# The sample's attention over quarters of the keys, with keys turned in 32x32 blocks by VectorE

## The chip, the cores and the metric

One core of a Trainium2 chip runs the whole program. The metric is the time of one execution in device microseconds; three runs of the kernel before took 3929.97, 3932.57 and 3942.89, their median is 3932.57 us.

## The reference

One step of a hybrid decoder layer: a prompt of 2048 rows and a sample group of 8 sequences with 4 new tokens each, both through the same weights. Only the sample's sparse attention matters here. For each of the 8 sequences it scores the 4 new tokens against 4096 cached keys, which lie in 32 pages of 128, and the 4 new ones; an indexer leaves 256 keys of 4100 to each token, the others get a score of minus infinity.

```python
s = jnp.einsum('bqkgd,bqnkd->bqkgn', qg, ks) * (A_HEAD_DIM ** -0.5)
s = jnp.where(valid[:, :, None, None, :], s, -jnp.inf)
p = jax.nn.softmax(s, axis=-1)
o = jnp.einsum('bqkgn,bqnkd->bqkgd', p, vs)
...
y_a = y_a * jax.nn.silu(zg_a)
```

There are 8 heads over 2 key heads of 64 features. A page holds, for each of its 128 keys, 128 floats of keys and 128 of values (both key heads), 1 KB a key, 128 KB a page. The kernel keeps all keys and adds to each score a bias that is 0 where the indexer selected the key and a very negative number elsewhere.

## The kernel before

The program is a row of stages, each closed by a barrier of all engines (`Stage.__exit__`, L100): the front (projections and indexer), the bias stage `stage_sample_bias` (L2331), the prompt's attention, the sample's attention `stage_sample_attend` (L2361), the prompt's RWKV, the sample's RWKV, and the merge. The change rewrites the second and the fourth of these; all else stays.

The bias stage has the indexer's selection as `part`, 128 partitions: 4 quarters of 1025 keys by 32 rows (8 sequences by 4 tokens). It copies the quarters side by side (L2352), turns them on TensorE in 33 pieces (L2345) and copies the result to `bias_t` with a key per partition (L2357).

The sample's attention goes sequence by sequence, in loops of the sequencers over two rounds of 4 buffers. A sequence's 32 pages come in through two queues, SyncE and GpSimd, 16 pages each: four page numbers are read from the table in SBUF into registers (L2398), then four DMAs follow (L2401). TensorE turns the 32 key blocks of 128x128 (L2444) in groups of four, ScalarE copies each group to SBUF as `kt` (L2485). For the scores (L2453) the turned keys of a page are the weights and the 32 query rows (4 tokens by 8 heads; zeros keep the key heads apart) are the 32 columns that stream, so a score has the key on the partition. VectorE adds the bias (L2524), takes the maximum over the pages (L2531); TensorE turns the maxima (L2458) and spreads the result over the partitions (L2460); VectorE subtracts (L2537), ScalarE takes the exp (L2489), VectorE sums (L2540). For the values (L2464) the probabilities of a page are the weights, 32 columns wide, and the page's values stream, 128 columns. A sequence's output is divided by its sum and the half of its own key head is kept (L2542 to L2546). After the last sequence GpSimd writes the output to DRAM and reads it back in another layout (L2427, L2429), TensorE turns it (L2472), and VectorE multiplies by the gate and writes `y_s` (L2553).

TensorE's order is written out for four sequences: the keys of sequence i + 1 are turned behind the scores of i, and the values of i follow behind that. Each engine works its list in order and waits on semaphores.

Of the kernel before, what the change touches and what calls it, by code (L numbers as in the profile page):

```python
# [16 lines left out]
NS = SB * ST  # L17
# [2313 lines left out]
def stage_sample_bias(nc, t, k, part, bias_t):  # L2331

    NPG = PAST // PAGE
    with Stage(nc, "sbi") as s:
        sc = s.sb("sc", [NS, L_S])
        turn = s.ps("turn", [P, 2048])
        step, joined, turned = s.sem("step"), s.sem("joined"), s.sem("turned")
        block = s.block()

        @block.tensor  # L2340
        def _(pe):
            pe.wait_ge(joined, 1)
            for c in range(NPG + 1):
                n = P if c < NPG else ST
                last = pe.transpose(turn[0:n, c * NS:(c + 1) * NS], sc[:, c * P:c * P + n], k.ident[0:NS, 0:NS])  # L2345
            last.then_inc(turned, 1)

        @block.vector
        def _(dve):
            chain = Chain(dve, step)  # L2350
            for at, keys in QUARTERS:
                chain.mark(dve.tensor_copy(sc[:, keys], part[at, :]))  # L2352
            chain.mark(dve.memset(bias_t[:, NPG, :], LOW))
            chain.catch_up()
            dve.sem_inc(joined, 1)
            dve.wait_ge(turned, 1)
            chain.mark(dve.tensor_copy(bias_t[:, 0:NPG, :], turn[:, 0:NPG * NS].rearrange("p (n c) -> p n c", c=NS)))  # L2357
            chain.link(dve.tensor_copy(bias_t[0:ST, NPG, :], turn[0:ST, NPG * NS:(NPG + 1) * NS]))


def stage_sample_attend(nc, t, k, z_s, bias_t, y_s):  # L2361

# [3 lines left out]
    NK = NPG + 1  # L2366
    BUFS = 4
    with Stage(nc, "sat") as s:
        oc = nc.dram_tensor("sat_oc", [SB, NS, HD], F32).ap()
        table = s.sb("table", [1, SB * NPG], I32)  # L2370
        kv = [s.sb(f"kv{i}", [P, NPG, 2 * P]) for i in range(BUFS)]
        kt = [s.sb(f"kt{i}", [P, NPG, P]) for i in range(2)]
        q_all, qb = s.sb("q_all", [P, SB, ST, KVH, G]), s.sb("qb", [P, NS])
        k_new, v_new = s.sb("k_new", [P, ST]), s.sb("v_new", [ST, SB, P])
        sm, pt = s.sb("sm", [P, NK, NS]), s.sb("pt", [P, NK, NS])
        mx, mrow, diag, top = s.sb("mx", [P, NS]), s.sb("mrow", [NS, 1]), s.sb("diag", [NS, NS]), s.sb("top", [P, NS])
        ones, v_b = s.sb("ones", [P, P]), s.sb("v_b", [ST, P])
        part, inv = s.sb("part", [P, NS]), s.sb("inv", [NS, 1])
        own, o_m, o = s.sb("own", [NS, P]), s.sb("o_m", [NS, P]), s.sb("o", [NS, SB, HD])
        row = s.sb("row", [NS, 1], I32)  # L2380
        rowf = s.sb("rowf", [NS, 1])
        ya, zg, th, gate = s.sb("ya", [NS, RW]), s.sb("zg", [P, 4, NS]), s.sb("th", [P, 4, NS]), s.sb("gate", [P, 4, NS])
        ptr = s.ps("ptr", [P, 1024])
        ps = s.ps("ps", [P, 1536])
        pm, po, pd = s.ps("pm"), s.ps("po"), s.ps("pd")
        tab_in, kv_in, kv_free, vn_in, made = s.sem("tab_in"), s.sems("kv_in", BUFS), s.sems("kv_free", BUFS), s.sem("vn_in"), s.sem("made")
        kv_in2 = s.sems("kv_in2", BUFS)
        sem = {n: s.sem(n) for n in ("set_up", "step", "qb_ok", "turned", "copied", "scored", "masked", "mxd", "mx_t", "dg",
                                     "topp", "cent", "expd", "summed", "pvd", "dend", "o_ok", "stored", "ya_in", "yt", "thd",
                                     "pages", "pages2")}  # L2390
        S = sem
# [3 lines left out]
        def load_pages(eng, done, it, i, half):  # L2395

            with eng.Fori(0, NPG // 8) as n:
                pages = [eng.value_load(table[0:1, bass.ds(it * (BUFS * NPG) + n * 4 + (i * NPG + half * (NPG // 2) + a), 1)],  # L2398
                                        min_val=0, max_val=NPH - 1) for a in range(4)]
                for a, page in enumerate(pages):  # L2400
                    eng.dma_start(kv[i][:, bass.ds(n * 4 + (half * (NPG // 2) + a), 1), :],  # L2401
                                  kv_rows[bass.ds(page, 1), :, :].rearrange("o p c -> p o c")).then_inc(done, 16)

        @block.sync
        def _(sp):
# [3 lines left out]
            for i in range(BUFS):  # L2409
                sp.sem_inc(kv_free[i], 1)  # L2410
            with sp.Fori(0, SB // BUFS) as it:
                for i in range(BUFS):
                    sp.wait_ge(kv_free[i], it + 1)
                    sp.sem_inc(S["pages"], 1)
                    load_pages(sp, kv_in[i], it, i, 0)
# [16 lines left out]
        def _(pe):  # L2432
            pe.wait_ge(S["set_up"], 1)
            pe.wait_ge(vn_in, 16)
            with pe.Fori(0, SB // BUFS) as it:
# [11 lines left out]
                for i in range(BUFS):  # L2447
# [7 lines left out]
                    if i + 1 < BUFS:  # L2455
                        turn(i + 1)
# [444 lines left out]
```

## Time and profile before

| | us |
|---|---|
| median of three runs | 3932.57 |
| the profiled execution | 3935.04 |
| its span in the profile | 3933.5 |
| PE busy | 3477.9 (88%) |
| DVE busy | 2146.5 (55%) |
| ACT busy | 1127.3 (29%) |
| POOL busy | 568.7 (14%) |

The span runs from the first to the last instruction of the profiled execution, and the 1.5 us beside it are the start and end of the execution. PE counts TensorE's matmuls, PEld its weight loads, which can run beside them. A float32 matmul leaves two records each of PE and PEld, one for each of its passes, a transpose one. PEclk is the clock that was granted to TensorE, as a share of 2.4 GHz. A row of a timeline merges neighbours of one form: "x64" are 64 records, and the time is that from the first start to the last end; the end of a matmul is modelled and holds the way through the array, which the next one overlaps.

### The profile page before, as it was taken

The page shows a single profiled execution, that of the slowest core. Times are in us where ns is not written, and L with a number is a line of the kernel's source. Part 1 is how long each engine was busy: PE and PEld are TensorE (multiplying, and loading weights), DVE is VectorE, ACT ScalarE, POOL GpSimd, SP SyncE. Part 2 cuts the span into 40 slices and gives each one's busy share as a digit, 9 for nine tenths or more (in the row PEclk, how much of TensorE's full clock was granted, in tenths as well). Part 3 has the DMA queues.
Part 4 walks back from the last instruction along what each step waited for, and adds up shares of the span by engine and source line. Part 5 has one row for each costly group of instructions (what it writes and reads, how often), then busy time and mean ns, then how long its engine had stood idle before and what let it go on. Part 6 is the DMA issues. An engine that isn't in the chain of part 4 may idle for free. (4 is left out here: it accounts for less than half of the span.)

```text
span 3933.5 us, 73267 instructions
## 1 busy us (share of the span) xinstructions
PE 3477.9 (88%) x29021; PEld 2124.0 (54%) x29021; DVE 2146.5 (55%) x4190; ACT 1127.3 (29%) x2375; POOL 568.7 (14%) x728
## 2 busy tenths in 40 slices
PE   8999999999999989999957858889871199999998
PEld 4444455555555545555547746667661165555653
DVE  2038899999999957666612235555543622222221
ACT  4236620000000004444411225555531021111221
POOL 3320000000000000000023013343432410000000
PEclk9999999999999998999966767666765599999999
DMA  4231111111111112110045111111114121111110
GB/s 147 69 104 46 39 56 53 60 55 58 55 59 54 60 55 54 25 25 17 7 132 171 43 31 38 43 39 39 37 22 175 36 77 62 56 58 60 48 48 22
DMA packets 209587, 229.62 MB, mean 58 GB/s; under 512 B 27178, under 2 KB 185317, under 8 KB 208773
## 3 DMA queue, kind: packets, MB, share of 16 engines
q1 hardware_dynamic: 150744, 119.10, 10.7%
q0 software_dynamic: 22672, 57.08, 5.2%
q10 hardware_dynamic: 35868, 49.13, 3.5%
q8 instruction: 224, 3.67, 0.4%
q14 instruction: 79, 0.64, 0.1%
HBM read 156.65 MB, written 68.59 MB: 57 GB/s over the span
## 5 line engine op out<-in xcount | busy, mean ns | idle before, releaser
L409 PE MATMUL fro_acc<-h_t,fro_w 128*128 128x416 f32 x3280 | 1174.2, 516 | 0.0
L409 PEld LDWEIGHTS fro_acc<-h_t,fro_w 128*128 128x128 f32 x3280 | 614.8, 190 | 542.6 <-issue 535.6
L692 DVE TENSOR_SCALAR_CACHE_REDUCE fro_work<-scores,fro_real 128x384 uint8<-128x384 f32 (+6 forms) x462 | 656.2, 1474 | 2.1
L516 ACT ACTIVATE fro_out<-fro_acc 128x416 f32<-128x416 f32 (+3 forms) x230 | 118.0, 513 | 794.6 <-PE fro_acc L409 711.8
L2786 DVE CUSTOM_DVE_ANT_0 att_seen<-att_ps,scores 128x512 f32<-128x512 f32 (+3 forms) x320 | 182.6, 608 | 119.9 <-PE att_ps L2675 119.3
L2021 PE MATMUL mrg_po<-wo,mrg_mrg 128*128 128x512 f32 (+1 forms) x544 | 236.5, 593 | 1.4 <-DVE mrg_mrg L2115 1.4
L2049 PE MATMUL mrg_pg<-wg,mrg_x_t 128*128 128x512 f32 (+1 forms) x544 | 236.3, 592 | 0.0
L658 DVE SCALAR_TENSOR_TENSOR scores<-fro_work,w_idx,scores 128x512 f32<-128x512 f32 (+3 forms) x280 | 187.9, 671 | 39.2 <-ACT fro_work L573 12.2
L2711 PE MATMUL att_po<-att_prob_t,att_v 128*64 128x128 f32 x2176 | 184.6, 288 | 2.1 <-ACT att_prob_t L2773 1.0
L2688 PE MATMUL att_pt<-ident,att_seen 128*128 128x128 f32 x1088 | 184.2, 291 | 1.5 <-ACT att_seen L2756 1.5
L2711 PEld LDWEIGHTS att_po<-att_prob_t,att_v 128*64 128x64 f32 x2176 | 113.9, 137 | 115.7 <-issue 83.0
L2675 PE MATMUL att_ps<-att_kt,att_qt 64*128 64x512 f32 (+3 forms) x640 | 164.5, 593 | 13.4 <-DMA att_qt<-z_t 13.4
L2021 PEld LDWEIGHTS mrg_po<-wo,mrg_mrg 128*128 128x128 f32 (+1 forms) x544 | 100.6, 185 | 134.4 <-issue 132.6
L573 ACT ACTIVATE fro_work<-fro_wk 128x512 f32<-128x512 f32 (+3 forms) x320 | 144.5, 540 | 90.9 <-PE fro_wk L482 90.0
L2049 PEld LDWEIGHTS mrg_pg<-wg,mrg_x_t 128*128 128x128 f32 (+1 forms) x544 | 100.6, 185 | 125.6 <-issue 124.8
L2756 ACT ACTIVATE att_seen<-att_seen,att_shift 128x128 f32<-128x128 f32 (+15 forms) x128 | 152.5, 1193 | 31.0 <-DVE att_shift L2794 29.9
L2121 DVE SCALAR_TENSOR_TENSOR mrg_th<-mrg_th,mrg_pw 128x1024 f32<-128x1024 f32 (+1 forms) x17 | 20.7, 1220 | 239.7 <-ACT mrg_th L2093 239.7
L2773 ACT ACTIVATE att_prob_t<-att_pt 128x512 f32<-128x512 f32 (+1 forms) x148 | 81.8, 553 | 242.2 <-PE att_pt L2688 242.2
L1990 POOL DMA_DIRECT2D mrg_m_in<-z_t x72 | 51.1, 710 | 678.7 <-DVE mrg_mrg L2115 676.0
L2688 PEld LDWEIGHTS att_pt<-ident,att_seen 128*128 128x128 f32 x1088 | 115.7, 142 | 56.5 <-issue 45.6
L2651 POOL MEMSET att_sel<- 8x512 f32 x1 | 0.5, 514 | 1004.5 <-POOLq L100 1004.5
L2005 PE MATMUL mrg_br<-mrg_y_in,wr 128*128 128x256 f32 (+2 forms) x576 | 126.4, 363 | 13.4 <-DMA mrg_y_in<-y_t 13.4
(428 smaller groups left out, 4947.4 us busy)
## 6 DMA issues: line engine op xcount, KB each, us to landing
z_t<-fro_out ACTq DMA_DIRECT2D x180, 208.0 KB
fro_w<-in_w_in SPq DMA_DIRECT2D x41, 512.0 KB, 4.2
sat_kv<-in_cache_kv SPq DMA_DIRECT2D x128, 128.0 KB, 2.3
sat_kv<-in_cache_kv POOLq DMA_DIRECT2D x128, 128.0 KB, 2.7
mrg_m_in<-z_t POOLq DMA_DIRECT2D x56, 256.0 KB, 3.2
z_t<-fro_out ACTq DMA_DIRECT2D x45, 192.0 KB
scores<-in_x_prompt SPq DMA_DIRECT2D x16, 512.0 KB, 8.3
mrg_x<-in_x_prompt SPq DMA_DIRECT2D x16, 512.0 KB, 3.4
```

The costliest lines, as they stand in the source:

```text
L409: last = pe.matmul(acc[e % 2][:, 0:CW], w[block_no % 3][:, kk, :], h_t[:, kk, CW * g:CW * g + CW], start=(kk == 0), stop=(kk == KD - 1))
L573: act.activation(rel[m % 8][:, 0:width], wk[m % 6][:, 0:width], ACT.Relu).then_inc(relued, 1)
L658: ins = dve.scalar_tensor_tensor(o, rel[m % 8][:, 0:width], wh, o, ALU.mult, ALU.add)
L692: chain.mark(dve.tensor_scalar(junk[b % 2][:, 0:n], scores[:, c:c + n], realf[:, b:b + 1], None, op, ALU.add, accum_out=count[:, b:b + 1]))
L2005: last = pe.matmul(br[:, d % 2, W * a:W * a + m], w[:, c, d * P:(d + 1) * P], y_in[g % 2][:, a, c, 0:m], start=(c == 0), stop=(c == 3))
L2021: last = pe.matmul(po[0:n, 512 * h:512 * h + 512], mrg[g % 2][:, c, o:o + n], wo[:, c, 512 * h:512 * h + 512], start=(c == 0), stop=(c == ...
L2049: last = pe.matmul(pg[0:n, 512 * h:512 * h + 512], x_t[:, c, 0:n], wg[:, c, 512 * h:512 * h + 512], start=(c == 0), stop=(c == KD - 1))
L2675: last = pe.matmul(ps[z % 2][e][:, 0:width], qt[b % 2][w, hh, :], kt[w, 512 * sl:512 * sl + width], start=True, stop=True)
L2688: last = pe.transpose(pt[i % 2][:, 256 * e + P * a:256 * e + P * a + P], seen[n % 3][e][:, P * kb:P * kb + P], k.ident[:, :])
L2711: last = pe.matmul(po[b % 2][64 * e:64 * e + 64, P * hh:P * hh + P], v[:, kb, 64 * e:64 * e + 64], prob_t[i % 4][:, 256 * e + P * a:256 * ...
L2756: act.activation(row, row, ACT.Exp, bias=shift[n % 3][:, e:e + 1], scale=scale, accum_out=total[b % 2][:, 4 * e + hh:4 * e + hh + 1]).then ...
L2786: dve.tensor_tensor_reduce(seen[n % 3][e][:, 512 * sl:512 * sl + width], ps[z % 2][e][:, 0:width], scores[:, c:c + width], 1.0, -3.4e38, A ...
```

## The change

The bias keeps its rows as partitions. A quarter of the 4096 keys belongs to each group of 32 partitions (rows (sequence, token)), so the bias stage only shifts the quarters of 1025 to quarters of 1024 and clamps them at -1e30; TensorE has no part in it.

The scores now have (quarter, token, head) on the 128 partitions and a quarter's 1024 keys on the free axis, in 4 banks of 256; a 257th column of each bank takes one of the 4 new keys. For a sequence, TensorE

- writes the bias to the score tile: 16 matmuls on the four diagonal 32x32 tiles, with a 0/1 matrix `sel` as weights that repeats a token's bias for its 8 heads;
- adds the scores: 64 matmuls with 32 query features as rows, 32 query rows as columns, and 256 keys streaming. The turned keys come from VectorE, which turns each 32x32 block where it stands, so that features lie on every group of 32 partitions; partition group n holds the keys 32n to 32n + 31 of every page, in every block f of 32 features;
- adds the new keys' scores (4 matmuls of one column).

VectorE takes one maximum per partition, over its own quarter alone; ScalarE takes one exp over all of it, which sums at once (`accum_out`). Nine transposes bring the probabilities to keys on partitions, ScalarE copies them, and the values are 32 matmuls on four column tiles, a quarter each. A sequence's four partial outputs are kept in `parts`. After the last sequence the quarters are weighed by the exp of their maximum against the row's, added by a matmul with four unit blocks (`same`), divided, and turned to `y_s` in SBUF, without the way through DRAM.

Three queues load the pages: of each quarter's 8 pages SyncE takes 3, GpSimd 3, ScalarE 2. There are 3 buffers of a whole sequence instead of 4, and one `kt` instead of two. The loops over sequences are written out. Numbers of lines in the order below are those of the changed file.

```diff
-            for at, keys in QUARTERS:
-                chain.mark(dve.tensor_copy(sc[:, keys], part[at, :]))
...
+            for g in range(4):
+                chain.mark(dve.tensor_scalar(whole[at[g], g:QK], part[at[g], 0:QK - g], FAR, None, ALU.max))
...
+            chain.mark(dve.tensor_copy(bias[:, :, 0:256].rearrange("p k (x i) -> p k x i", i=32),
+                                       whole[:, 0:QK].rearrange("p (x k i) -> p k x i", k=4, i=32)))
...
-    BUFS = 4
+    BUFS = 3
+    GP = NPG // 4
+    SHARE = (slice(0, 3), slice(3, 6), slice(6, 8))
...
+        def load_pages(eng, b, who):
+            i, mine = b % BUFS, SHARE[who]
+            if b >= BUFS:
+                eng.wait_ge(weighed, b - BUFS + 1)
+                eng.wait_ge(turned, 4 * (b - BUFS) + 4)
+            for g in range(4):
+                at = [GP * g + a for a in range(mine.start, mine.stop)]
+                pages = [eng.value_load(table[0:1, NPG * b + a:NPG * b + a + 1], min_val=0, max_val=NPH - 1) for a in at]
...
         @block.tensor
...
+                pe.transpose(po[0:ST, 256:256 + P], prob_n[b % 2][:, :], k.ident[:, :]).then_inc(flip_n, 1)
+                for x in range(GP):
+                    last = pe.transpose(tp[:, P * x:P * x + P], prob[b % 2][:, x, :, :].rearrange("p k i -> p (k i)"), k.ident[:, :])
...
+                pe.wait_ge(copied, 3 * b + 3)
+                for x in range(GP):
+                    for g in range(4):
+                        pe.matmul(po[rows(g), 0:P], pt[:, x, rows(g)], kv[i][:, GP * g + x, P:2 * P], start=(x == 0),
+                                  stop=(x == GP - 1 and g < 3), skip_group_check=True)
...
+            for b in range(SB):
+                if b:
+                    pe.wait_ge(exped, b)
+                    pe.wait_ge(exp_n, b)
+                for n in range(4):
+                    for g in range(4):
+                        last = pe.matmul(ps[rows(g), n, 0:257], sel[rows(g), ST * b:ST * b + ST, :].rearrange("p t h -> p (t h)"),
+                                         bias[rows(g), n, :], start=True, stop=False, skip_group_check=True)
...
+                if b:
+                    weigh(b - 1)
...
+                for g in range(4):
+                    pe.wait_ge(turned, 4 * b + g + 1)
+                    for f in range(4):
+                        for n in range(4):
+                            pe.matmul(ps[rows(g), n, 0:256], qd[rows(n), b, f, :], kt[rows(n), GP * g:GP * g + GP, 32 * f:32 * f + 32],
+                                      start=False, stop=(f == 3), skip_group_check=True)
...
         @block.scalar
...
+            for b in range(SB):
+                act.wait_ge(peaked, b + 1)
+                act.activation(prob[b % 2][:, :, :, :].rearrange("p x k i -> p k x i"), ps[:, :, 0:256].rearrange("p k (x i) -> p k x i", i=32),
+                               ACT.Exp, bias=less[:, b:b + 1], scale=float(HD ** -0.5), accum_out=sum_a[:, b:b + 1]).then_inc(exped, 1)
...
+                if b + 2 < SB:
+                    load_pages(act, b + 2, 2)
...
         @block.vector
...
+                    if b and g == 0:
+                        dve.wait_ge(scored, b)
+                    dve.transpose(kt[:, GP * g:GP * g + GP, :], kv[b % BUFS][:, GP * g:GP * g + GP, 0:P]).then_inc(turned, 1)
+                if b:
+                    keep(b - 1)
+                dve.wait_ge(scored, b + 1)
+                chain.link(dve.tensor_reduce(most[:, b:b + 1], ps[:, :, 0:257], AX.XY, ALU.max))
+                dve.tensor_scalar(less[:, b:b + 1], most[:, b:b + 1], -float(HD ** -0.5), None, ALU.mult).then_inc(peaked, 1)
```

TensorE's list before, from the last keys of a sequence to the scores of the next (`sat_ptr` holds turned keys, `sat_ps` scores, `sat_pm` maxima, `sat_po` outputs; ISA and REGISTER_ALU rows set registers of the loop):

```order
L2444 MATMUL sat_ptr<-ident,sat_kv 128x128 x4
L2458 MATMUL sat_pm<-ident,sat_mx 32x128
L2460 MATMUL sat_pm<-sat_diag,sat_ones 128x32
L2461 REGISTER_ALU
L2462 ISA
L2464 MATMUL sat_po<-sat_kv,sat_pt 32x128 x32
L2465 MATMUL sat_po<-sat_v_b,sat_pt 32x128
L2469 MATMUL sat_pd<-sat_ones,sat_part 32x1
L2449 REGISTER_ALU
L2451 ISA
L2453 MATMUL sat_ps<-sat_qb,sat_kt 128x32 x32
L2454 MATMUL sat_ps<-sat_qb,sat_k_new 4x32
```

The same list now, the first sequence's scores, then the second's bias, the first's values, and the second's scores (`sat_tp` holds turned probabilities):

```order
L2453 MATMUL sat_ps<-bias_t,sat_sel 32x257 x16
L2463 MATMUL sat_ps<-sat_kt,sat_qd 32x256 x64
L2466 MATMUL sat_ps<-z_s,sat_qf 32x1 x4
L2453 MATMUL sat_ps<-bias_t,sat_sel 32x257 x16
L2432 MATMUL sat_po<-ident,sat_prob_n 4x128
L2434 MATMUL sat_tp<-ident,sat_prob 128x128 x8
L2440 MATMUL sat_po<-sat_kv,sat_pt 32x128 x32
L2442 MATMUL sat_po<-sat_v_new,sat_pt_n 32x128
L2463 MATMUL sat_ps<-sat_kt,sat_qd 32x256 x64
```

The key turning has left TensorE, the 32 wide score matmuls became 16 + 64 small ones, and the values of a sequence stand between the bias and the scores of the next.

ScalarE's list now, from a sequence's exp to the first of the eight page loads for the sequence after the next (before, it held eight copies of turned keys and an exp, and no DMA):

```order
L2494 ACTIVATE sat_prob,sat_sum_a<-sat_ps,sat_less 128x4x8x32
L2496 ACTIVATE sat_prob_n,sat_sum_b<-sat_ps,sat_less 128x4
L2501 ACTIVATE sat_pt_n<-sat_po 4x128
L2504 ACTIVATE sat_pt<-sat_tp 128x512 x2
L2403 TENSOR_LOAD sat_table
L2403 ISA x2
L2403 TENSOR_LOAD sat_table
L2403 ISA x2
L2405 ISA
L2405 DMA sat_kv<-in_cache_kv 128x256
```

The loads moved to a queue that also holds the exp of the next sequence, behind them.

## Rows read from the trace of the kernel before

**Rows 1.** Windows: us, busy (count) of PE, PEld, DVE, ACT, POOL, PEclk, DMA share, GB/s.
```profile
1993.70:2314.60 320.90, 228.98 (x1356) 205.15 (x1356) 71.11 (x131) 45.85 (x73) 70.08 (x131) 0.69 0.35 105
1998.80:2021.50 22.70, 0.00 (x0) 0.00 (x0) 0.49 (x3) 0.00 (x0) 8.66 (x17) 0.50 0.61 186
...
2208.70:2221.00 12.30, 12.25 (x66) 12.13 (x66) 0.00 (x0) 0.00 (x0) 0.00 (x0) 0.58 0.00 0
2231.20:2240.00 8.80, 8.78 (x65) 8.04 (x66) 1.85 (x1) 0.00 (x0) 0.00 (x0) 0.81 0.00 0
2362.00:2364.00 2.00, 1.92 (x64) 1.69 (x64) 0.11 (x2) 1.99 (x5) 0.00 (x0) 0.50 0.15 42
```

**Rows 2.** Timeline of one sample: start us, us, engine line op out<-in.
```profile
2208.75 12.17 PE L2453 MATMUL sat_ps<-sat_qb,sat_kt 128*128 128x32 f32 x64 [2.22 <-DVEq L2520]
...
2221.06 6.25 PE L2444 MATMUL sat_ptr<-ident,sat_kv 128*128 128x128 f32 x32
2221.36 1.23 DVE L2524 TENSOR_TENSOR sat_sm<-sat_ps,bias_t 128x1024 f32<-128x1024 f32 x1 [12.90 <-PE sat_ps L2454]
...
2222.70 1.97 DVE L2531 TENSOR_REDUCE sat_mx<-sat_sm 128x32 f32<-128x1056 f32 x1
...
2230.01 1.08 ACT L2489 ACTIVATE sat_pt<-sat_sm 128x1056 f32<-128x1056 f32 x1 [2.07 <-DVE sat_sm L2537]
...
2231.22 8.76 PE L2464 MATMUL sat_po<-sat_kv,sat_pt 128*32 128x128 f32 x64 [2.77 <-ACT sat_pt L2489]
...
2242.88 12.17 PE L2453 MATMUL sat_ps<-sat_qb,sat_kt 128*128 128x32 f32 x64 [2.22 <-DVEq L2520]
```

**Rows 3.** Timeline of the page loads on SyncE and GpSimd.
```profile
1998.76 111.36 SPq L2401 DMA_DIRECT2D sat_kv<-in_cache_kv  x82
...
2004.43 2.48 POOL L2401 DMA_DIRECT2D sat_kv<-in_cache_kv  x4 [3.10 <-issue]
2009.98 2.48 POOL L2401 DMA_DIRECT2D sat_kv<-in_cache_kv  x4 [3.06 <-issue]
```

**Rows 4.** Timeline of the stage's end.
```profile
2307.88 0.15 DVE L2542 RECIPROCAL sat_inv<-sat_pd 32x1 f32<-32x1 f32 x1 [8.69 <-PE sat_pd L2469]
...
2314.25 0.29 DVE L2553 SCALAR_TENSOR_TENSOR y_s<-sat_pd,sat_gate 128x128 f32<-128x128 f32 x1 [4.88 <-PE sat_pd L2472]
```

**Rows 5.** Costliest groups on VectorE: shapes, count, busy us, mean ns, idle.
```profile
L1744 DVE STREAM_TRANSPOSE rwk_pw<-rwk_ta 128x256 f32<-128x256 f32 x64 | 28.0, 437 | 58.5 <-ACT rwk_ta L1542 58.5
```

**Rows 6.** Chain that ended last, in the merge: start us, us.
```profile
3200.96 13.73 PE mrg_pg L2049 x32
```

**Rows 7.** Timeline of TensorE, four stretches with small tiles.
```profile
188.34 1.14 PE L445 MATMUL fro_wk<-fro_work,fro_qs 32*32 32x512 f32 x32
...
227.20 3.74 PE L461 MATMUL fro_wk<-scores,fro_sel 128*32 128x512 f32 x48
...
299.81 1.14 PE L482 MATMUL fro_wk<-fro_work,fro_qi 32*128 32x512 f32 x8
300.88 2.36 PE L409 MATMUL fro_acc<-h_t,fro_w 128*128 128x416 f32 x6
...
2362.08 1.93 PE L1312 MATMUL rwk_zz<-rwk_ta,rwk_pw 32*32 32x64 f32 x64 [1.86 <-DVE rwk_pw L1744]
```

**Rows 8.** Timeline of ScalarE in the prompt's attention.
```profile
1950.42 0.60 ACT L2773 ACTIVATE att_prob_t<-att_pt 128x512 f32<-128x512 f32 x1 [1.64 <-PE att_pt L2688]
...
1951.00 2.00 ACT L2756 ACTIVATE att_seen<-att_seen,att_shift 128x2048 f32<-128x2048 f32 x1
...
1952.91 0.19 ACT L2756 ACTIVATION_READ_ACCUMULATOR att_seen<-att_seen,att_shift 128x1 f32 x1
```

**Rows 9.** Timeline of the bias stage.
```profile
1456.74 2.83 DVE L2352 COPY sbi_sc<-part 32x1025 f32<-32x1025 f32 x4 [27.67 <-PEq L100]
...
1463.43 1.22 DVE L2357 COPY bias_t<-sbi_turn 128x1024 f32<-128x1024 f32 x1 [3.82 <-PE sbi_turn L2345]
```

**Rows 10.** Tile sat_po: min/median/max ns, first and last start.
```profile
L2464 PEld LDWEIGHTS sat_po<-sat_kv,sat_pt x512: 109/110/178, 2055.0 to 2306.8; 128*32 128x32 f32 x171
```

More of the change, by code:

```diff
@@ L2328, in _, with stage_sample_bias @@
             g.finish(dve, 0, y_s[0][:, :, :])
-def stage_sample_bias(nc, t, k, part, bias_t):
-    NPG = PAST // PAGE
+FAR = -1.0e30
+def stage_sample_bias(nc, t, k, part, bias):
+    QK = PAST // 4
     with Stage(nc, "sbi") as s:
-        sc = s.sb("sc", [NS, L_S])
-        turn = s.ps("turn", [P, 2048])
-        step, joined, turned = s.sem("step"), s.sem("joined"), s.sem("turned")
+        whole = s.sb("whole", [P, QK + ST])
+        step = s.sem("step")
         block = s.block()
[L2340 to L2346, printed above, removed]
         @block.vector
@@ L2386, in stage_sample_attend @@
[L2386 to L2391, printed above, removed]
+        kt = s.sb("kt", [P, NPG, P])
@@ new lines, in stage_sample_attend @@
+        qd, qf, sel = s.sb("qd", [P, SB, 4, NS]), s.sb("qf", [P, SB, ST, KVH, G]), s.sb("sel", [P, SB * ST, AH])
+        v_new = s.sb("v_new", [ST, SB, P])
+        prob, prob_n = [s.sb(f"prob{i}", [P, GP, 4, 32]) for i in range(2)], [s.sb(f"prob_n{i}", [P, ST]) for i in range(2)]
+        pt, pt_n = s.sb("pt", [P, GP, P]), s.sb("pt_n", [ST, P])
+        most, less, sum_a, sum_b = s.sb("most", [P, SB]), s.sb("less", [P, SB]), s.sb("sum_a", [P, SB]), s.sb("sum_b", [P, SB])
+        parts, same = s.sb("parts", [P, SB, P]), s.sb("same", [P, NS])
@@ L2392, in stage_sample_attend, with rows @@
         block = s.block()
         kv_rows = t["cache_kv"][0].rearrange("n p a h d -> n p (a h d)")
[L2395 to L2402, printed above, removed]
+        def rows(g):
+            return slice(32 * g, 32 * g + 32)
@@ L2408, in _ @@
             sp.wait_ge(tab_in, 16)
[L2409 to L2415, printed above, removed]
+            for b in range(SB):
+                load_pages(sp, b, 0)
         @block.gpsimd
@@ new lines, in _ @@
+            weigh(SB - 1)
+            pe.wait_ge(peaked, SB)
+            pe.transpose(end[0:SB, 0:P], most[:, :], k.ident[:, :]).then_inc(m_turned, 1)
+            pe.wait_ge(peak_ok, 2)
+            pe.matmul(end[:, 256:256 + SB], peaks[:, :, :].rearrange("b g q -> b (g q)"), k.ident[0:SB, 0:SB], start=True, stop=True)\
+              .then_inc(spread, 1)
+            pe.wait_ge(all_w, 3)
+            for h in range(2):
+                pe.matmul(tp[0:NS, 512 * h:512 * h + 512], same[:, :], parts[:, 4 * h:4 * h + 4, :].rearrange("p b c -> p (b c)"),
+                          start=True, stop=True)
@@ L2507, in _ @@
+            chain.catch_up()
+            for n in range(1, 4):
+                chain.mark(dve.tensor_copy(qd[rows(n), :, :, :], qd[0:32, :, :, :]))
             dve.wait_ge(made, 1)
```

261 lines of the change are left out of this document (120 added, 141 removed).

## The prediction

> **What bounds the kernel now.** I read the table of windows first, to see how much of the span the edited stage holds and which engine fills it. The sample's attention runs from 1993.7 to 2314.6 us, 321 us of 3933.5; TensorE is busy for 229 of them, at a mean granted clock of 0.69, between its two levels of 1.2 and 2.4 GHz, and the DMA engines for 0.35 [rows 1]. A stage is closed by a barrier of all engines, so what the stage loses the kernel loses: nothing of another stage runs beside it.
>
> The timeline of one sample comes next, after the DMAs are over [rows 2]. Seen from one row L2453 to the next, 2208.75 to 2242.88, a sample takes 34.1 us, and its parts stand one after another: scores 12.17, turning the next sample's keys 6.25, then maximum, subtraction and exp on VectorE and ScalarE, values 8.76. The scores are 32 matmuls of only 32 columns (64 records: every float32 matmul leaves two, its two passes). They bring a full 128x128 weight each, and PEld is busy for 12.13 of 12.30 us [rows 1]. So they are paid in weight loads.
>
> The third view is the page loads [rows 3]. GpSimd issues four pages in 5.55 us (2004.43 to 2009.98), 1.39 a page, SyncE 82 in 111.4, 1.36 a page. A sample of 32 pages over two queues thus takes 16 x 1.39 = 22 us. The first waits for it (1998.8 to 2021.5, TensorE idle, DMA share 0.61 [rows 1]), the others don't, since 34 is more than 22.
>
> **The change part by part.** Removed per sample are TensorE's key turning with its eight copies, the 64 records of scores, the 64 of values, VectorE's sum pass and column maxima, the transposes of the maxima. Per stage goes the round trip of the output through DRAM, part of the 6 us from L2542 to y_s [rows 4]. Added is the following, per sample.
>
> *Turned keys.* Four VectorE transposes of 128x1024. The trace has the same operation at 128x256, 437 ns [rows 5]; its first 1024-column neighbour is L2524, 1.23 us for 1024 elements. I take 437 + 768 x (1230 / 1024) ns = 1.36, ends 1.23 and 4 x 0.437 = 1.75, so 5.4 us. They begin when the scores before them are read and the maximum is taken (the key buffer is single), 1.4 us into the cycle, and end at 6.8. TensorE asks for them at 11 or later, so they cost nothing; at 1.75 apiece they end at 8.4 and still do not.
>
> *TensorE.* The price of a pass is that of L2049: 32 records of 512 columns in 13.73 us, 0.429 each, 0.84 ns a column at full clock [rows 6]. The question is how many tiles share a pass. Four 32-row matmuls of 512 columns (eight records of L482) take 1.14 us; one after another they would take 8 x 0.429 = 3.4. Sixteen 32x32 matmuls (32 records of L445) also take 1.14. Four 32-column tiles under all 128 rows (L461, 48 records) take 3.74 for eight rounds of 512 columns, which is 0.43 a round plus 0.3 for sixteen one-column records [rows 7]. So tiles that differ in rows or columns run together, and I count rounds:
> - bias, 16 matmuls of 257 columns on the four diagonal tiles: 4 rounds x 2 passes x 257 x 0.84 ns = 1.7 us;
> - scores, 64 of 256 columns. Within a group of output rows the four row tiles run together, but the four feature blocks follow each other on the same tile: 16 rounds x 2 x 256 x 0.84 = 6.9. Were all 16 tiles fed at once it would be 1.7, were none shared 27.5; L445 and L482 were issued so that no tile came twice, hence the middle;
> - nine transposes of 128 columns in one pass, 1.0; values, 8 rounds x 2 x 128 x 0.84 = 1.7, and 0.1 for the new tokens; the four one-column matmuls 0.3;
> - changes of tile shape. From L482 (299.81) to the next L409 (300.88) are 1.07, where two passes are 0.86, so 0.2 out and back; some 0.15 each, five of them, 0.7.
>
> That is 12.4 us at full clock, 24.8 at half. At the stage's present mean of 0.69 it is 18.0. I take that: the new matmuls stream more columns per weight load, which speaks for more, and the waits below speak for less. Before, the values, which stream 128 columns, ran at 0.81 and the scores at 0.58 [rows 1].
>
> *Where TensorE waits.* The score tile is single too, so from the last score to the next bias stand VectorE's maximum over 1028 PSUM columns (1.23, as L2524; at the 1.97 of L2531 at the dearest), the scaling 0.17, an exp of 1024 (half of L2756's 2.00 us), its accumulator read 0.19, the small exp with its own read 0.4, and four hand-overs of 0.1 (L2489 ends at 2231.09, L2464 begins at 2231.22): 3.4 us [rows 2, 8]. After the transposes it waits for ScalarE's last copy, 0.60 (L2773), and hand-overs, 1.0. So 4.4, and a cycle is 18.0 + 4.4 = 22.4 us.
>
> *Queues.* SyncE and GpSimd now issue 12 pages a sample and ScalarE 8. At the old price that is 12 x 1.39 = 16.7 us, under 22.4; the share of DMA time would rise from 0.61 at 22 us a sample to 0.8. ScalarE's 8 pages, 11.1 us, stand in its queue behind the copies and ahead of the next exp. That is covered by the values (2.6 at this clock), the scores (10) and the maximum (1.4), 14 us; without that cover the next exp is late by the difference.
>
> *Bias stage.* It has four copies from 1456.74 (2.83 us), 33 transposes on TensorE, and from 1463.43 the copies back, which end at 1464.7 [rows 9], so 8 us. The new one stays on VectorE: four passes like the four copies, seven tiny ones (0.1 each), one copy of 1024 (1.22): 5 us, 3 less.
>
> *Sum.* The first sample's pages are in after 16.7 + 2 us, at 2018; its last quarter of turning (1.4) and of scores (3.5 at the half clock that the idle engine has there, 0.50 [rows 1]) ends at about 2023. Seven cycles of 22.4 are 157. Then 3.4 for exp, 1.0 for the copy, (1.0 + 1.8 + 0.4) / 0.69 = 4.7 for the last values. The join is a chain of some 16 short steps: two VectorE passes of 1024 (1.25 each), three of 512 (0.6), four 512-column records (0.86 to 1.7), eight transposes and nine steps of 0.2 to 0.4 with hand-overs, 11 us, 4 more than the old end. y_s is written at 2023 + 157 + 9 + 11 = 2200 instead of 2314.5, 114 less; with the bias stage 117. The profiled execution took 3935.0, so 3818; the median of the runs shown is 2.5 lower, so **3816**. Two prices that no row shows: clearing more semaphores at the stage's end (0 to 1 us), and fetching code that is now written out rather than looped (0, by L445, which is written out too and puts 32 loads and 32 matmuls into 1.14 us; at the most the 0.3 that L461 has over its rounds, per sample [rows 7]).
>
> **A rule against the change.** Consecutive score rounds load new weights into the same tiles. L1312 does just this, eight times two passes on four tiles with 64 columns: 64 records in 1.93 us [rows 7] at a granted clock of 0.50 [rows 1], where 16 passes x 64 columns x 1.67 ns are 1.71. What is left, 0.22, is paid once, not per pass, so the loads are hidden and my sum has none. The Trainium skill, TensorE: Matmul & The Clock Gate, Part 3 on packing, says that a weight load overlaps matmuls in flight only where its row group is another; by that the 32 score passes would each show theirs. The trace disagrees, in that row.
>
> **The rivals.**
> 1. *The clock stays at half.* For it: 4.4 us of waits in each cycle, and L1312 at 0.50. Then 24.8 + 4.4 = 29.2, seven are 204, and 2024 + 204 + 24 = 2252: 65 less, **3867**. Against it: the values' 0.81.
> 2. *The clock is full, and the queues bound.* 12.4 + 4.4 = 16.8 against 16.7 of issuing; 2023 + 118 + 18 = 2159, 159 less, **3774**. For it: the merge's L2049 streams at full clock; against it, the waits.
> 3. *Weight loads stand between the passes.* A load of 32 columns takes 0.11 us, 0.18 at the longest (L2464 on PEld [rows 10]); 32 of them are 3.5 to 5.7 a sample, 25 to 40 over seven, **3848**. Against it: L1312. It is what the skill's rule above would give.
> 4. *Slower: tiles on the same output rows do not share a pass.* The four row tiles of a score round add into the same partitions, in four banks, round after round, and no row of before accumulates so. Then the scores are 64 x 2 x 0.215 = 27.5, TensorE 33.0 / 0.69 = 47.8, a cycle 52.2, the stage ends at 2413, **4027**. It decides from a cycle of 39 us on, where 2023 + 7 x 39.2 + 20 meets 2317.5. Against it: L445 and L482 put four row tiles on the same output partitions and shared.
>
> **How the numbers follow.** The forecast has 0.47, rival 1 0.17, rival 2 0.18, rival 3 0.05, rival 4 0.06. Some 0.05 goes to stalls that leave a gain of 15 to 60 us (ScalarE's loads holding back the exp), 0.02 to none. Under 0.3%, 12 us, no change can be told. So faster 0.92, same 0.02, slower 0.06. From rival 2 to rival 1, rounded outward: 3770 to 3870, with the rest and half a case left out.
>
> **What would show it.** Right: score starts 21 to 24 us apart, a score group of 64 matmuls in 7 to 12 us, four transposes of about 1.3 each that end before the values, VectorE's maximum directly behind the scores, TensorE idle for 3 to 4 us before the bias. Wrong: a score group near 27 us or more, TensorE waiting for sat_kt or the DMAs in every sample, exp waiting for ScalarE's own loads, a gap before each round.

## The result and the profile after

The changed kernel takes **3762.5 us** (median of four runs, 3750.74 to 3766.32), the kernel before beside it 3933.5: a ratio of 0.9554, 95% interval 0.9532 to 0.9576. It is faster by 171 us where the prediction had 117, and below the range's low end of 3770. The profiled execution of the changed kernel took 3759.72, its span is 3758.1.

First the windows of the changed kernel, with the columns of [rows 1]: the stage, seven samples, then one sample's scores, one bias, and the scores behind it.

```profile
1984.60:2139.00 154.40, 103.26 (x1961) 66.14 (x1961) 67.55 (x112) 23.28 (x58) 52.41 (x97) 0.83 0.69 220
2009.00:2120.00 111.00, 82.77 (x1713) 55.27 (x1709) 46.53 (x50) 19.96 (x49) 41.92 (x78) 0.88 0.78 248
2019.66:2024.50 4.84, 4.84 (x135) 3.11 (x132) 0.29 (x1) 0.00 (x0) 2.89 (x6) 1.00 0.90 286
2027.99:2031.00 3.01, 3.01 (x32) 1.48 (x32) 1.74 (x2) 0.00 (x0) 1.17 (x3) 0.51 1.00 334
2035.00:2040.00 5.00, 5.00 (x139) 3.24 (x136) 0.29 (x1) 0.00 (x0) 1.77 (x4) 1.00 0.95 296
```

The stage takes 154 us instead of 321. TensorE is busy for 103 of them instead of 229, the granted clock is 0.83 instead of 0.69, and within the samples 0.88: 1.00 in the scores, 0.51 in the bias shown.

One sample on TensorE, from the last score of one to the last score of the next (timeline of the changed kernel, columns as in [rows 2]):

```profile
2024.46 0.41 PE L2466 MATMUL sat_ps<-z_s,sat_qf 128*32 128x1 f32 x8
2027.97 3.36 PE L2453 MATMUL sat_ps<-bias_t,sat_sel 32*32 32x257 f32 x32 [3.10 <-ACT sat_prob_n L2496]
2031.27 0.27 PE L2432 MATMUL sat_po<-ident,sat_prob_n 128*4 128x128 f32 x1
2031.38 1.04 PE L2434 MATMUL sat_tp<-ident,sat_prob 128*128 128x128 f32 x8
2033.15 1.95 PE L2440 MATMUL sat_po<-sat_kv,sat_pt 128*32 128x128 f32 x64 [0.74 <-ACT sat_pt L2504]
2035.03 0.29 PE L2442 MATMUL sat_po<-sat_v_new,sat_pt_n 4*32 4x128 f32 x1
2035.04 0.42 PE L2463 MATMUL sat_ps<-sat_kt,sat_qd 32*32 32x256 f32 x4
...
2035.28 4.62 PE L2463 MATMUL sat_ps<-sat_kt,sat_qd 32*32 32x256 f32 x124
2039.84 0.41 PE L2466 MATMUL sat_ps<-z_s,sat_qf 128*32 128x1 f32 x8
```

It takes 15.4 us here, 15.6 in the mean of seven (2009.09 to 2118.41), where [rows 2] have 34.1. In order: new keys 0.41, wait for the exp 3.10, bias 3.30, transposes 1.14, wait for the copies 0.74, values 1.89, scores 4.80.

In this sample the transposes behind the bias run at full clock, 1.04 us. In three of the other six they don't, and in a fourth only in part; the slowest pair is this:

```profile
2059.34 3.65 PE L2453 MATMUL sat_ps<-bias_t,sat_sel 32*32 32x257 f32 x32 [3.08 <-ACT sat_prob_n L2496]
...
2063.09 1.91 PE L2434 MATMUL sat_tp<-ident,sat_prob 128*128 128x128 f32 x8
```

From the bias's start to the end of the transposes are 4.4 to 5.7 us over the seven samples, 4.65 in the mean.

VectorE and ScalarE in the same sample:

```profile
2024.91 1.23 DVE L2550 TENSOR_REDUCE sat_most<-sat_ps 128x1 f32<-128x1028 f32 x1 [4.53 <-PE sat_ps L2466]
2026.17 0.15 DVE L2551 TENSOR_SCALAR sat_less<-sat_most 128x1 f32<-128x1 f32 x1
2026.35 2.37 DVE L2546 STREAM_TRANSPOSE sat_kt<-sat_kv 128x1024 f32<-128x1024 f32 x2
2029.99 1.25 DVE L2546 STREAM_TRANSPOSE sat_kt<-sat_kv 128x1024 f32<-128x1024 f32 x1 [1.27 <-DMA sat_kv<-in_cache_kv]
2032.96 1.25 DVE L2546 STREAM_TRANSPOSE sat_kt<-sat_kv 128x1024 f32<-128x1024 f32 x1 [1.72 <-DMA sat_kv<-in_cache_kv]
```
```profile
2032.01 1.09 ACT L2504 ACTIVATE sat_pt<-sat_tp 128x512 f32<-128x512 f32 x2 [0.17 <-PE sat_tp L2434]
2033.71 8.48 ACTq L2405 DMA_DIRECT2D sat_kv<-in_cache_kv  x8
2042.23 1.11 ACT L2494 ACTIVATE sat_prob<-sat_ps,sat_less 128x1024 f32<-128x1024 f32 x1 [9.14 <-DVE sat_less L2551]
```

A transpose takes 1.2 to 1.25 us. The third and the fourth wait for pages, yet the fourth ends at 2034.21, before the scores begin. ScalarE's eight page loads end at 2042.19, though the maximum was ready at 2041.70: this exp is half a microsecond late. SyncE issues all its pages in one row, 96 in 108.68 us, 1.13 a page against the 1.36 of [rows 3]:

```profile
1987.96 108.68 SPq L2405 DMA_DIRECT2D sat_kv<-in_cache_kv  x96
```

The bias stage runs from 1454.21 to 1458.68, 4.5 us instead of 8, all of it on VectorE. The end, in the chain of the last sample (y_s against [rows 4]):

```profile
2118.41 0.41 PE L2466 MATMUL sat_ps<-z_s,sat_qf 128*32 128x1 f32 x8
...
2123.75 3.27 PE L2440 MATMUL sat_po<-sat_kv,sat_pt 128*32 128x128 f32 x64 [0.74 <-ACT sat_pt L2504]
...
2138.35 0.61 DVE L2582 TENSOR_TENSOR y_s<-sat_po,sat_gate 64x128 f32<-64x128 f32 x2 [1.15 <-PE sat_po L2482]
```

From the last score to y_s are 20.5 us; the join is 11.6 of them.

Two readings follow. TensorE's own sequence, waits included, sets the sample, and pages and transposes lie beside it; and the scores are cheaper than 16 rounds one after another (4.8 us, not 6.9), because the four groups of output rows overlap. A rival: the pages bound the sample, and TensorE's gain is theirs. All edits below are to the changed kernel unless said otherwise. "Stage" is the time from the load of the page table to the end of y_s, "sample" the mean distance of the last scores; for the changed kernel 154.3 and 15.6 us. Stage and sample are read from one profiled execution of each kernel; ratios are to the kernel before.

### The profile page after: what moved, and what is told of

It is laid out like the page before. It is cut to its first block and busy times, and to the rows that moved or that the text cites. A ratio compares the mean times of both kernels' runs of the same rounds, so it can differ in the third digit from the quotient of the medians.

```text
span 3758.1 us, 73685 instructions
## 1 busy us (share of the span) xinstructions
PE 3342.4 (89%) x29593; PEld 1977.7 (53%) x29593; DVE 2133.7 (57%) x4177; ACT 1103.7 (29%) x2360; POOL 550.3 (15%) x694
```

## The experiments

**Scores with the output-row group innermost.**

```diff
-for g in range(4):
-    pe.wait_ge(turned, 4 * b + g + 1)
-    for f in range(4):
-        for n in range(4):
+pe.wait_ge(turned, 4 * b + 4)
+for f in range(4):
+    for n in range(4):
+        for g in range(4):
             pe.matmul(ps[rows(g), n, 0:256], ...
```


> Edit: the scores wait for all four turned groups, and then run with the output-row group innermost, so that 16 different 32x32 tiles come before one comes twice. Theory A (TensorE's own sequence bounds a sample, and a group of scores starts only as far ahead of the one before as the order of issue lets it: the four groups of the changed kernel start 1.0 us apart and each needs 8 x 0.216 = 1.7 us): the 128 score passes take 2.0 to 2.4 us instead of 4.7, the time from one sample's end of scores to the next falls from 15.6 us to 13.3, the last sample's end by 2.6; the first sample loses up to 2 us because it waits for all its pages. Together 7 x 2.3 + 2.6 - 2 = 17 us less: 3746 us. Theory B (the pages and their VectorE transposes bound a sample, TensorE only waits elsewhere): the scores shorten, but TensorE then waits for sat_kt as long, and the time stays within 4 us of 3762. Theory C (matmuls on the same four output rows share nothing across row groups): the scores stay at 4.7 us or lengthen.

Measured: 3768.0 us, ratio 0.9574 (0.9549 to 0.9598); stage 154.6, sample 15.3. Its timelines of TensorE and ScalarE:

```profile
2040.00 0.51 PE L2463 MATMUL sat_ps<-sat_kt,sat_qd 32*32 32x256 f32 x14
...
2040.24 2.69 PE L2463 MATMUL sat_ps<-sat_kt,sat_qd 32*32 32x256 f32 x114
2042.85 0.41 PE L2466 MATMUL sat_ps<-z_s,sat_qf 128*32 128x1 f32 x8
2047.40 3.65 PE L2453 MATMUL sat_ps<-bias_t,sat_sel 32*32 32x257 f32 x32 [4.14 <-ACT sat_prob_n L2496]
```
```profile
2038.67 7.09 ACTq L2405 DMA_DIRECT2D sat_kv<-in_cache_kv  x8
2045.81 1.11 ACT L2494 ACTIVATE sat_prob<-sat_ps,sat_less 128x1024 f32<-128x1024 f32 x1 [7.75 <-issue]
```

The scores fall to 2.9 us, so tiles of all rows and columns run together. (In two of the seven samples they take 3.5 and 4.0, since TensorE stands still for 0.6 us inside them; why, the profile does not show.) The time doesn't fall, for three reasons. The wait before the bias grows from 3.1 to 4.1 here, and by 0.4 to 1.3 in six of the seven samples, since ScalarE is still issuing pages when the maximum is ready at 2044.72. More of the bias then runs at half clock: it takes 3.5 us in the mean of seven, 3.0 before. And the first sample, which now waits for all its pages, ends 2.3 us later. Theory A was right on the scores and wrong on the time; theory B named no such wait.

**Scores one group after another.**

```diff
-                      start=False, stop=(f == 3), skip_group_check=True)
+                      start=False, stop=(f == 3), skip_group_check=True).then_inc(ended, 1)
+    pe.wait_ge(ended, 64 * b + 16 * g + 16)
```


> Edit: each group of scores waits until every matmul of the group before has ended. This is what the prediction counted with (16 rounds x 2 passes = 6.9 us at full clock). Theory A (TensorE's sequence bounds a sample, the overlap of the groups is worth 6.9 + waits - 4.7): four groups of 1.73 us plus about 0.2 us for each wait = 7.7 us, the sample 3.0 us longer, 8 x 3.0 = 24 us more: 3786 us. Theory B (pages and transposes bound): they take up most of it, under 8 us more.

Measured: 3795.5 us, ratio 0.9654 (0.9632 to 0.9676); stage 182.4, sample 19.5.

```profile
2042.33 1.93 PE L2464 MATMUL sat_ps<-sat_kt,sat_qd 32*32 32x256 f32 x32 [0.17 <-PE sat_ps L2464]
2044.42 1.93 PE L2464 MATMUL sat_ps<-sat_kt,sat_qd 32*32 32x256 f32 x32 [0.17 <-PE sat_ps L2464]
```

A group is 2.1 us with its wait, four are 8.4 instead of 4.8. The sample grows by 3.9 us and the stage by 28.1, where 24 were expected: what TensorE loses, the stage loses in full. That is theory A. The median rises by 33 us, or by 27 against the changed kernel's repetition below (3768.2).

**Filler in TensorE's wait, 12 matmuls.** Their results are not used.

```diff
 if b:
+    for _ in range(12):
+        pe.matmul(end[0:32, 0:256], k.ident[:, 0:32], bias[:, 0, 0:256], start=True, stop=True)
     pe.wait_ge(exped, b)
```


> Edit: where TensorE waits for the exponential of the sample before (3.1 to 3.6 us), it first runs 12 matmuls of 256 columns into a bank that is unused until the end; their results are not used. Theory A (the granted clock falls to half because TensorE itself stood still just before): the fillers take 12 x 0.215 = 2.6 us inside the wait, the granted clock stays 1.00 through the bias, whose matmuls take 1.75 us instead of 2.5 to 3.6: 1.2 us less per sample, 8 us in all: 3754 us, and the clock of the stage over 0.95. Theory B (the clock falls for another cause, the DMA traffic or the small transposes): segments of half clock remain, the fillers take up to 5.2 us, outlast the wait by 2 us, and the time is up to 14 us longer.

Measured: 3763.6 us, ratio 0.9569 (0.9548 to 0.9589); stage 156.4, sample 15.9. Windows of seven samples, and of one bias:

```profile
2006.00:2118.00 112.00, 106.83 (x1889) 65.57 (x1881) 45.03 (x49) 19.63 (x49) 41.92 (x78) 1.00 0.78 247
...
2043.68:2045.60 1.92, 1.92 (x34) 0.95 (x34) 1.21 (x1) 0.00 (x0) 0.60 (x2) 1.00 0.93 307
```

The clock is 1.00 throughout, with the same DMA share of 0.78 as before the edit: the half clock is the price of TensorE's own wait, not of the transfers. The bias takes 1.9 us and the transposes 1.04, in every sample. Each filler, though, cost two passes of 0.215, which the expectation had counted as one: 5.1 us in a wait of 3.1.

**Filler, 6 matmuls**, the same edit with `range(6)`, beside a later repetition of it and of the changed kernel.

> Edit: the filler of the third run with 6 matmuls instead of 12. In that run each of the 12 took two passes of 0.215 us, 5.1 us in all, 2.1 us more than the wait of 3.08 it was to fill, while the granted clock was 1.00 from the first sample to the last and the bias took 1.94 us. Theory A (the half clock is the price of TensorE's own wait, and TensorE's sequence bounds a sample): 6 x 0.43 = 2.6 us fits into the wait, the bias takes 1.94 us instead of 2.5 to 3.6 and the transposes 1.04 instead of up to 1.9: 1.3 us less per sample, 15.6 to 14.3, 9 us in all: 3753 us. Theory B (2.6 us of filler leave the clock as it was, or what is won is lost in another wait, as ScalarE's page loads that now end just before its exponential is due): within 3 us of 3762.

> The changed kernel again, unchanged, as the base of the next run on the same chip: 3762 us, within 8.

> The kernel of the fifth run again (6 fillers in TensorE's wait), beside the changed kernel on the same chip. Theory A (its stage of 141.9 us against 154.3 is what the time shows): 12 us below the changed kernel. Theory B (the difference of 3751 and 3762 was between chips): within 4 us.

Measured: 3750.9 us, ratio 0.9540 (0.9507 to 0.9573), then 3753.0, 0.9535 (0.9515 to 0.9555), with the changed kernel at 3768.2, 0.9564 (0.9540 to 0.9588), on the same chip. Stage 141.9 and 142.2, sample 13.9. Window of seven samples and one cycle's fill and bias, in the repetition:

```profile
2010.70:2122.00 111.30, 96.00 (x1871) 61.97 (x1868) 49.68 (x59) 22.75 (x57) 42.05 (x78) 0.97 0.77 246
```
```profile
2038.69 2.54 PE L2450 MATMUL sat_end<-bias_t,ident 128*32 128x256 f32 x11
2041.80 1.94 PE L2455 MATMUL sat_ps<-bias_t,sat_sel 32*32 32x257 f32 x32 [0.56 <-ACT sat_prob_n L2498]
```

Theory A: 12 us less in the stage, 15 between the medians. That is 0.4%, and the two ratios' intervals overlap; but the five runs each on one chip lie at 3745.2 to 3757.6 and at 3752.9 to 3781.5, and the stage is shorter by the same 12 us in both profiles. The sample loses 1.7 us: 1.15 in the bias, 0.5 in the transposes. In the repeated changed kernel's own profile the stage was 158.8, 4.5 more than in the first. Three exps stood behind ScalarE's eight loads, which took 8.1 to 9.0 us there, and came 1.7 us late in all, 1.2 more than in the first profile; bias and transposes met more half clock, 2.1 us over the seven samples; and from the last score to y_s are 1.3 us more, with the last transposes at half clock too.

**Group innermost, and ScalarE's loads split.** The first sample keeps the old order; ScalarE issues two of its pages between exp and copies, where it waits 4 us for TensorE, and six behind (the last argument names the quarters).

```diff
 ...
+if b + 2 < SB:
+    load_pages(act, b + 2, 2, range(1))
 act.wait_ge(flip_n, b + 1)
 ...
-    load_pages(act, b + 2, 2)
+    load_pages(act, b + 2, 2, range(1, 4))
```


> Edit: scores with the output-row group innermost as in the first run, except for the first sample, which keeps the order of the changed kernel; and of the 8 pages that ScalarE issues per sample two go between its exponentials and its copies, where it waits about 4 us for TensorE, six stay behind the copies. In the first run the scores fell from 4.7 to 3.2 us, but ScalarE issued its 8 pages for 7.1 us and more and came to the exponential 1.0 us late, so TensorE waited 4.0 to 4.1 us instead of 3.08, and the first sample came 3.9 us later. Theory A (that is where the gain went): the wait is 3.1 us again, the sample takes 15.6 - 1.5 = 14.1 us, the first one comes as in the changed kernel: 7 x 1.5 = 10 us less: 3752 us. Theory B (the pages bound a sample, at 12 x 1.13 = 13.6 us of SP's and POOL's issue and the transfers behind it): waits for sat_kt appear, and the gain is under 4 us.

> Edit: only the split of ScalarE's pages (two between exponentials and copies, six behind), the scores as in the changed kernel. In the changed kernel ScalarE's loads delayed the exponential in one sample of eight, by 0.5 us. Theory A (the loads there are hidden): no change, within 3 us of 3762. Theory B (ScalarE's loads hold the samples already in the changed kernel): 5 us less or more.

Measured: 3757.9 us, ratio 0.9556 (0.9522 to 0.9589), stage 144.2, sample 14.4. The split alone: 3766.4, 0.9574 (0.9539 to 0.9609), stage 153.7, sample 15.4, no change. With both edits the stage is 10 us shorter, and the wait before the bias is 3.1 again in six of the seven samples. (Between the medians are 4.6 us, 10.3 against the repetition.) So the scores' gain reaches the stage once the loads are out of the exp's way; the missing wait was ScalarE's queue. The split alone also leaves a caution: behind the same wait, its second sample's bias shows no half clock at all.

```profile
2012.27 1.94 PE L2453 MATMUL sat_ps<-bias_t,sat_sel 32*32 32x257 f32 x32 [3.08 <-ACT sat_prob_n L2496]
```

**Both, with the filler.**

> Edit: the sixth kernel with the 6 filler matmuls. Theory A (both gains are TensorE's and add until a queue bounds): TensorE's sequence is 15.6 - 1.5 - 1.3 = 12.8 us, below the 13.6 us that SP and POOL need for their 12 pages: a sample takes 13.6 us, with short waits for sat_kt: 7 x 2.0 = 14 us less than the changed kernel: 3748 us. Theory B (the two do not add since ScalarE's stream bounds: 1.8 exponentials + 1.5 copies + 8 pages + waits): 14.1 us, 3752 us.

Measured: 3753.7 us, ratio 0.9530 (0.9496 to 0.9565); stage 141.4, sample 13.55. Waits of TensorE, us in total, times, longest, and the window of seven samples:

```profile
PE sat_ps L2469 <- DVE sat_kt L2554: 8.2, 7, 1.9
PE sat_po L2440 <- ACT sat_pt L2512: 5.2, 7, 0.7
PE sat_ps L2455 <- ACT sat_prob_n L2502: 4.0, 7, 0.6
```
```profile
2012.80:2107.00 94.20, 76.31 (x1773) 49.60 (x1783) 45.59 (x49) 19.62 (x49) 41.92 (x78) 1.00 0.91 291
```

Here TensorE waits for turned keys in every sample, at 13.55 us, which is 12 pages at 1.13: the pages bound, and the two gains do not add. It is their issuing rather than the transfers: SyncE's 96 pages take 107 us there at a DMA share of 0.91, and 109 in the changed kernel at 0.78. Against the six fillers alone its median is no lower.

**Two queues.** ScalarE issues no pages, SyncE and GpSimd 16 each.

```diff
-SHARE = (slice(0, 3), slice(3, 6), slice(6, 8))
+SHARE = (slice(0, 4), slice(4, 8))
 ...
-load_pages(act, 0, 2)
-load_pages(act, 1, 2)
 ...
-if b + 2 < SB:
-    load_pages(act, b + 2, 2)
```


> Edit: ScalarE issues no pages; SP and POOL issue 16 pages of each sample each, as in the kernel before, but still written out without loops. Theory A (a queue's own issue, 1.12 to 1.14 us a page, would bound the samples as soon as it is over 15.6 us): 16 x 1.13 = 18.1 us per sample, so the last pages land 8 x 18.1 + 7 = 152 us after the stage's start instead of 112, TensorE waits for sat_kt in most samples, and the end of the stage moves from 154 us to about 175: 20 us more, 3782 us. Theory B (the transfers themselves, not the issue, set when pages land): two queues bring them as fast, within 5 us of 3762. Theory C (the loads in ScalarE's stream delay its copies and exponentials): without them the waits for sat_pt and sat_prob_n shrink, and the time is less.

Measured: 3788.5 us, ratio 0.9627 (0.9606 to 0.9649); stage 178.7, sample 18.2. GpSimd's pages and TensorE's waits:

```profile
2055.30 2.30 POOL L2405 DMA_DIRECT2D sat_kv<-in_cache_kv  x4 [2.24 <-issue]
2059.84 2.29 POOL L2405 DMA_DIRECT2D sat_kv<-in_cache_kv  x4 [2.24 <-issue]
```
```profile
PE sat_ps L2453 <- ACT sat_prob_n L2494: 21.6, 7, 3.1
PE sat_ps L2463 <- DVE sat_kt L2542: 13.7, 6, 4.0
```

Four pages take 4.54 us, 1.135 each, and 16 of them 18.2: the sample to the tenth. Theory A.

**The kernel before, its page loads written out.**

```diff
-with eng.Fori(0, NPG // 8) as n:
+for n in range(NPG // 8):
 ...
```


> Edit, to the kernel before: its page loads are written out without loops, on the same two queues. Theory A (the loop made an issue 1.36 to 1.39 us instead of 1.13, and in the kernel before that only delays the first sample): SP's 16 pages of the first sample take 18 us instead of 22, the first sample and with it the whole stage end 4 us earlier, every later sample stays at 34.1 us: 3929 us against 3933. Theory B (the third queue, not the missing loop, made the issue cheaper): 1.36 us a page and no change. Theory C (the pages bound the samples of the kernel before): a sample shorter by up to 16 x 0.25 = 4 us, 28 us in all.

Measured: 3927.8 us, ratio 0.9979 (0.9959 to 0.9999), the same time. GpSimd's pages:

```profile
2006.43 2.30 POOL L2402 DMA_DIRECT2D sat_kv<-in_cache_kv  x4 [2.25 <-issue]
2010.98 2.30 POOL L2402 DMA_DIRECT2D sat_kv<-in_cache_kv  x4 [2.26 <-issue]
```

The price is theory A's: four pages in 4.55 us, 1.14 each, with two queues, so the loop was the dear part. The first keys are turned 4.1 us earlier after the stage's start (23.7 us against 27.8). But the profile's stage is no shorter: from the page table to the last sample's values 313.6 us against 313.4. The windows of 107 us from about the first scores on, of this kernel and of the one before, differ in the clock:

```profile
2024.00:2131.00 107.00, 91.74 (x495) 82.84 (x496) 23.89 (x36) 17.50 (x27) 38.82 (x72) 0.63 0.59 179
```
```profile
2028.00:2135.00 107.00, 85.23 (x509) 76.81 (x507) 23.84 (x36) 17.66 (x29) 40.21 (x75) 0.71 0.63 186
```

The early start met more half clock, 0.63 against 0.71, in the one profile of each; that this is what took the 4.1 us is argued from it and not shown. What the median's 8 us are, at the edge of its interval, stays open.

**Short score matmuls.** Each of 256 columns becomes four of 64.

```diff
-pe.matmul(ps[rows(g), n, 0:256], ..., kt[rows(n), GP * g:GP * g + GP, ...
+for h in range(4):
+    pe.matmul(ps[rows(g), n, 64 * h:64 * h + 64], ..., kt[rows(n), GP * g + 2 * h:GP * g + 2 * h + 2, ...
```


> Edit, to the changed kernel: each score matmul of 256 columns becomes four of 64 columns, the same products in 4 times as many instructions, 512 passes each with its weight load instead of 128. In the kernel before the granted clock fell to half inside matmuls of 32 columns, though TensorE had no wait there. Theory A (the clock falls also through many short matmuls without a wait, and that made the 0.69 with which the prediction divided): segments of half clock inside the scores, which take over 13 us per sample. Theory B (only TensorE's waits lower it): 1.00 throughout the scores, which take 512 passes at the 25 ns that the first run shows between starts, 12.8 us, or less: a sample of 21 to 24 us, the time about 3820 us.

Measured, one run: 3885.3 us. The first sample's scores, then windows of the scores of two later samples:

```profile
1998.46 28.36 PE L2464 MATMUL sat_ps<-sat_kt,sat_qd 32*32 32x64 f32 x512
```
```profile
2038.20:2054.50 16.30, 16.30 (x514) 16.25 (x510) 0.29 (x1) 0.00 (x0) 6.47 (x12) 1.00 0.80 250
2103.00:2115.90 12.90, 12.90 (x236) 12.76 (x232) 0.00 (x0) 0.00 (x0) 2.74 (x6) 0.50 0.47 152
```

Neither theory holds whole. 16 us of short matmuls without a gap ran at 1.00, in four of the seven samples after the first, so shortness alone did not lower the clock here. In the later sample shown TensorE stood still for 0.70 us in the middle of its scores, at 2101.2; it was then at half and stayed there through the short matmuls to the end of the group, where the changed kernel is back at full behind its bias. Two other samples did the same behind standstills of 0.26 and 1.48 us. And the first sample's scores began at half, after the wait for pages, and stayed at 0.50 for 28 us without a gap; the changed kernel's first scores ran at 0.83 in their first 3.3 us. The expectation's remark that the kernel before has no wait there was wrong: its scores follow 2.22 us of waiting [rows 2]. The passes are 32 ns apart at full clock, not 25, and the half clock comes on top: hence the larger time.

## Why the prediction was wrong, point by point

The sign, the mechanism and most prices were right, and of the signs named beforehand the wait before the bias, the maximum and the transposes came as told. Starts of 21 to 24 us and a score group of 7 to 12 did not: 15.6 and 4.8. What failed is the sentence "At the stage's present mean of 0.69 it is 18.0", and behind it "16 rounds x 2 x 256 x 0.84 = 6.9". A sample was to take 22.4 us and takes 15.6; seven of them are 47.5 of the 54 us missed.

- **TensorE's clock.** The forecast added 5.6 us to 12.4 for the clock. In the row by row sample the bias alone runs at half, 3.30 us against the 1.9 of the filler runs: 1.4 us. Over the seven samples, with the transposes that it reaches too, it is 1.6: bias and transposes take 3.02 and 1.63 in the mean, and 1.87 and 1.15 in the filler runs. So 4.0 us of the 6.8 are the clock's. The mean of 0.69 belonged to the old work: a wait, then 12 us of 32-column matmuls at 0.58 [rows 1, 2]. Those were what the change removed. The filler runs show the rest: with the wait filled, no half clock behind it. I weighed "more columns per weight load" and "the waits" against each other and kept the old mean, instead of asking stretch by stretch what TensorE would do.
- **The scores.** 4.8 us at full clock, not 6.9: 2.1 us. The first two experiments bracket it, 8.4 with the groups kept apart and 2.9 with all 16 tiles fed in turn. The three figures that the prediction named, 1.7, 6.9 and 27.5, were the right scale, but a group begins before the one before it has ended, which L445 and L482 do not show.
- **Changes of tile shape.** 0.7 us forecast, a term to which nothing here corresponds: the rows follow each other without a gap.
- **Waits.** 4.4 forecast, 3.10 + 0.74 = 3.84 measured, 0.5 less. The hand-overs are short, and the exp takes 1.11.
- **Other matmuls.** Bias 1.7 (1.9 at full), transposes 1.0 (1.14), values 1.8 (1.89), new keys 0.3 (0.41): right, each a little too low, 0.5 in all. With the clock's 4.0, the scores' 2.1, the shapes' 0.7 and the waits' 0.5 that makes the 6.8.
- **Turned keys.** 1.36 each forecast, 1.2 to 1.25 measured, ending before the scores want them, though held by pages, not by the maximum.
- **Queues.** "At the old price" was wrong: 1.13 us a page instead of 1.39, since the loop is gone (the two runs with two queues each). It makes 13.6 us a sample instead of 16.7. The first sample's scores end 24.9 us into the stage instead of 29.3: 4.4 us of the miss, of which 12 x 0.26 = 3.1 are the issuing. Rival 2, at 3774, came closest, with the clock full but for the bias and some transposes. But it had 16.8 us a sample even so, and 16.7 from the queues; the 15.6 measured lie below both, so the scores and the page's price carried the time out of the range, not the clock alone. Its bound, at the new price, is reached in the run that joins both edits.
- **ScalarE's loads.** Named as a danger, covered by "14 us". They are just covered: late by 0.5 us in one sample of the changed kernel, and by 0.4 to 1.3 in six of seven as soon as the scores are shorter.
- **Bias stage and end.** 3 us forecast, 3.5 measured; 20 from the last score to y_s, 20.5 measured; the join 11 and 11.6. From y_s to the next stage's first instruction are 1.3 us, 2.5 in the kernel before: the price for clearing more semaphores, which no row showed, did not appear.
- **Rivals.** Weight loads between the passes (rival 3, the Trainium skill's rule in TensorE: Matmul & The Clock Gate, Part 3): the trace disagrees again. In the run with the groups apart the eight passes that each of four tiles makes with a new weight each take 1.93 us, where 8 x 0.215 are 1.72; the 0.2 left is paid once a group, not once a pass. Rival 4: tiles on the same output rows do share; the first experiment has all 16 at work.

## What to carry to other kernels

A stage's mean granted clock is no constant to divide new work by: split the new sequence into stretches, and charge half clock only to the stretch behind a wait like those that the trace shows with it, as a range: the same 3.1 us of waiting cost between nothing and 2.6 us here. When a chain becomes shorter, look at once for what stands in the queues beside it: here the scores gave 1.7 us a sample in the mean, of which ScalarE's own page loads took 0.7 and a longer half clock in the bias 0.5; with two of eight loads moved to where ScalarE waits, and the first sample left in its old order, the sample was 1.2 us shorter instead of 0.3. And a wait that cannot be removed can still be kept from slowing what follows it: six throw-away matmuls in it made each sample 1.7 us shorter.

## What was not expected of the hardware

- Four row tiles of 32x32 that add into the same output rows, in four banks, share their passes, and so do all 16 tiles: 128 passes of 0.215 us in 2.9 us.
- TensorE after a wait of 3.1 us ran its next 3 us at 0.51 in the sample shown; with that wait filled for 2.6 us the clock was 0.97 over seven samples, filled whole 1.00, at DMA shares of 0.77 to 0.78. Behind the same wait the loss varied: bias and transposes took 4.4 to 5.7 us in the changed kernel, and 3.0, as with the wait filled, in one sample of the run with the split alone.
- Passes of 64 columns without a gap kept the clock that they began with: 16 us at 1.00, 28 us at 0.50.
- A page read into a register and a DMA issued cost 1.13 us on SyncE and GpSimd written out, 1.36 to 1.39 in a loop of the sequencer. ScalarE took 0.9 to 1.1.
